# Attention values with the value block as weights: two heads' probabilities streamed, scaled by their sums before they are turned

## What is computed

```python
m = jnp.maximum(jnp.max(scores, axis=-1, keepdims=True), sink)
pexp = jnp.exp(scores - m)
probs = pexp / (jnp.sum(pexp, axis=-1, keepdims=True) + jnp.exp(sink - m))
out = jnp.einsum('bgrnqk,bnkgd->bnqgrd', probs.astype(v.dtype), vv)
```

## Time and profile before

| | us |
|---|---|
| median of three runs | 2171.71 |
| lowest, highest | 2169.91, 2173.41 |
| the profiled execution, its own time | 2171.98 |
| its span, first to last instruction | 2170.4 |

### The profile page before, as it was taken

One profiled execution on the slowest core, in us unless ns is written; L12 is line 12 of the kernel. 1 busy time (PEld: TensorE's weight loads), 2 busy tenths in 40 slices (PEclk: granted clock), 3 DMA queues, 4 the chain that ended last, 5 costly groups with the idle time before them and its releaser, 6 DMA issues. The chain is left out here.

```text
span 2170.4 us, 29183 instructions
## 1 busy us (share of the span) xinstructions
PE 2090.3 (96%) x10250; PEld 1740.3 (80%) x10250; DVE 1308.9 (60%) x1828; ACT 844.2 (39%) x1589; POOL 601.2 (28%) x604
## 2 busy tenths in 40 slices
PE   7999999979999999999979999999999999999997
PEld 6888889968878878878858888888888888878885
DVE  6854543227777767767743344558877777752523
ACT  5332221114455454454443222435444443443432
POOL 1000011135576566565610000014222222100000
PEclk9999999989999999999989999999999999999998
DMA  6223252223344343443355434322222222355343
GB/s 218 68 90 97 78 174 100 78 93 129 110 125 131 119 119 124 123 126 96 101 173 174 137 136 144 131 88 76 88 83 69 80 87 87 136 163 195 111 151 88
DMA packets 131838, 254.80 MB, mean 117 GB/s; under 512 B 25328, under 2 KB 70512, under 8 KB 131728
## 3 DMA queue, kind: packets, MB, share of 16 engines
q1 hardware_dynamic: 85584, 174.98, 25.1%
q0 software_dynamic: 15936, 57.42, 7.8%
q10 hardware_dynamic: 30208, 20.98, 3.0%
HBM read 189.63 MB, written 63.70 MB: 117 GB/s over the span
## 5 line engine op out<-in xcount | busy, mean ns | idle before, releaser
L155 PE MATMUL ps_zg<-u_hi,g_hi 128*128 128x512 f32 x448 | 185.6, 414 | 0.0
L157 PE MATMUL ps_zg<-u_hi,g_lo 128*128 128x512 f32 x448 | 176.7, 394 | 0.0
L156 PE MATMUL ps_zg<-u_lo,g_hi 128*128 128x512 f32 x448 | 175.5, 392 | 0.0
L2051 DVE TENSOR_TENSOR lt_d_lo<-lt_w_raw,lt_d_hi 128x640 fp32r<-128x640 f32 (+1 forms) x64 | 57.1, 892 | 147.4 <-ACT lt_d_hi L1776 142.3
L967 POOL TENSOR_TENSOR mx_seg<-mx_seg,mx_cbm 128x1024 f32<-128x1024 f32 x32 | 76.0, 2376 | 161.1 <-DVE mx_cbm L1124 161.1
L155 PE MATMUL lt_ps<-lt_h_hi,lt_w_hi 128*128 128x512 f32 x256 | 100.8, 394 | 15.0 <-DVE lt_h_lo L2089 13.9
L155 PE MATMUL ps_zg<-z_w,u_hi 128*128 128x512 f32 x256 | 107.7, 421 | 7.1 <-DVE mx_silu L1149 6.5
L157 PE MATMUL ps_zg<-z_w,u_lo 128*128 128x512 f32 x256 | 101.8, 398 | 0.0
L1650 POOL TENSOR_TENSOR lt_t_f<-lt_w_raw 128x512 f32<-128x512 f32 x21 | 29.1, 1385 | 261.7 <-DVE lt_t_lo L1979 260.2
L1776 ACT ACTIVATE lt_d_hi<-lt_w_raw 128x640 fp32r<-128x640 f32 (+1 forms) x64 | 50.6, 791 | 130.5 <-PE lt_ps L157 111.5
L156 PE MATMUL ps_zg<-z_w,u_hi 128*128 128x512 f32 x256 | 101.1, 395 | 0.0
(11 more groups left out here) (390 smaller groups left out, 6237.9 us busy)
## 6 DMA issues: line engine op xcount, KB each, us to landing
lt_w_raw<-in_w_up SPq DMA_DIRECT2D x44, 512.0 KB, 4.5
mx_a_row<-acs_s SPq DMA_DIRECT2D x32, 512.0 KB, 3.9
g_raw<-in_w_xbc SPq DMA_DIRECT2D x24, 512.0 KB, 3.7
tok_s<-fr_work POOLq DMA_DIRECT2D x24, 512.0 KB, 4.0
lt_sig<-gate_s SPq DMA_DIRECT2D x24, 512.0 KB, 3.6
lt_w_raw<-in_w_down SPq DMA_DIRECT2D x32, 384.0 KB, 3.2
ff_s<-lt_fo SPq DMA_DIRECT2D x21, 512.0 KB, 5.1
lt_w_raw<-in_w_down SPq DMA_DIRECT2D x32, 320.0 KB, 2.9
```

What stands on the lines that cost most here:

```text
L155: pe.matmul(dst, s_hi, m_hi, start=first, stop=False)
L156: pe.matmul(dst, s_hi, m_lo, start=False, stop=False)
L157: return pe.matmul(dst, s_lo, m_hi, start=False, stop=last)
L2051: dve.tensor_tensor(d_lo[:, m % 2, 0:n], w_raw[:, m % 2, 0:n], d_hi[:, m % 2, 0:n].bitcast(F32), ALU.subtract).then_inc(dw_lo_done, 1)
```

## The change

The value product is turned round. The value block (64 columns) becomes the weights, and the transposed probabilities of two heads (256 columns) are streamed; two such products write the partitions 0 to 63 and 64 to 127 of `ps_f`. The result has the features on the partitions, which is the form in which it is stored, so `o_tok`, its transposes (L1255) and `attention_out` go. The division by the sums can no longer come after the product as a scale per partition: it moves ahead of the transposes of the probabilities, as four `tensor_scalar` on `sc` with a pointer to each head's reciprocal sum, in `scale_probabilities`, which VectorE runs behind the state update and ahead of L1164. TensorE's wait for `exp_done` becomes one for `p_scaled`; its waits for `o_ready` go.

```diff
+            def scale_probabilities(n, keys, own):
+
+                dve.wait_ge(sink_done, n + 1)
+                own.did(dve.tensor_tensor(rden[:], sums[:], sink_e[:], ALU.add))
+                own.wait()
+                own.did(dve.reciprocal(rden[:], rden[:]))
+                own.wait()
+                for r in range(REP):
+                    ins = dve.tensor_scalar(sc[:, r, 0:keys], sc[:, r, 0:keys], rden[:, r:r + 1], None, ALU.mult)
+                ins.then_inc(p_scaled, 1)
...
-                    if not opening:
-                        attention_out(n - 1, first and c == 1)
...
                         dve.tensor_tensor(state[:], kept[:], ps_f[:], ALU.add).then_inc(state_ready, 1)
+                    scale_probabilities(n, keys, own)
                     dve.wait_ge(diag_done, n + 1)
...
-                    dve.wait_ge(sink_done, n + 1)
-                    do(dve.tensor_tensor(rden[:], sums[:], sink_e[:], ALU.add))
-                    do(dve.reciprocal(rden[:], rden[:]))
...
             def values(g, c):
 
-                pe.wait_ge(p_ready, NT * g + c + 1)
+                n = NT * g + c
+                pe.wait_ge(p_ready, n + 1)
+                if c < NT - 1:
+                    pe.wait_ge(state_ready, (NT - 1) * g + c + 1)
+                else:
+                    pe.wait_ge(o_out, n)
                 j, blocks = c % 2, 1 if c == 0 else 2
-                for r in range(REP):
-                    for b in range(blocks):
-                        block_of = c if b == j else c - 1
-                        last = pe.matmul(ps_a[:, r * HD:(r + 1) * HD], p_t[:, r, b], v_in[:, block_of % 4],
+                for b in range(blocks):
+                    block_of = c if b == j else c - 1
+                    for h in range(2):
+                        last = pe.matmul(ps_f[h * HD:(h + 1) * HD, 0:2 * P].rearrange("p (a n) -> p a n", a=2),
+                                         v_in[:, block_of % 4], p_t[:, 2 * h:2 * h + 2, b],
                                          start=(b == 0), stop=(b == blocks - 1))
                 last.then_inc(pv_done, 1)
...
-                pe.wait_ge(o_ready, n + 1)
-                if c < NT - 1:
-                    pe.wait_ge(state_ready, (NT - 1) * g + c + 1)
-                else:
-                    pe.wait_ge(o_out, n)
-                for a in range(2):
-                    last = pe.transpose(ps_f[:, a * P:(a + 1) * P], o_tok[:, a * P:(a + 1) * P], ident[:])
-                last.then_inc(o_turned, 1)
...
-                    pe.wait_ge(exp_done, n + 1)
+                    pe.wait_ge(p_scaled, n + 1)
```

More of the change, by code:

```diff
@@ L825, in mixers @@
         p_t = s.sb("p_t", [P, REP, 2, P])
-        o_tok = s.sb("o_tok", [P, REP * HD])
         o_t = s.sb("o_t", [P, 2, 2, P])
@@ L847, in mixers @@
             s.sem(n) for n in "gated sq_done v_ready r0_ready yn_ready y_turned y_out".split())
-        rotated, qk_turned, q_ready, scored, masked, max_ready, exp_done, sink_done, p_turned, p_ready, pv_done, o_ready, o_turned, o_out = (
-            s.sem(n) for n in "rotated qk_turned q_ready scored masked max_ready exp_done sink_done p_turned p_ready pv_done o_ready o_turned o_out".split())
+        rotated, qk_turned, q_ready, scored, masked, max_ready, sink_done, p_scaled, p_turned, p_ready, pv_done, o_out = (
+            s.sem(n) for n in "rotated qk_turned q_ready scored masked max_ready sink_done p_scaled p_turned p_ready pv_done o_out".split())
         dve_own, pool_own, act_own = s.sem("dve_own"), s.sem("pool_own"), s.sem("act_own")
@@ L993, in outputs @@
                 act.activation(y_t[:, j], ps_e[:].rearrange("p (a n) -> p a n", a=4), ACT.Copy).then_inc(y_out, 1)
-                act.wait_ge(o_turned, n + 1)
+                act.wait_ge(pv_done, n + 1)
                 if not opening:
@@ L1045, in group @@
                     for r in range(REP):
-                        ins = act.activation(sc[:, r, 0:keys], sc[:, r, 0:keys], ACT.Exp, bias=negm[:, r:r + 1],
-                                             accum_out=sums[:, r:r + 1])
-                    ins.then_inc(exp_done, 1)
+                        act.activation(sc[:, r, 0:keys], sc[:, r, 0:keys], ACT.Exp, bias=negm[:, r:r + 1],
+                                       accum_out=sums[:, r:r + 1])
                     act.activation(sink_e[:], mx[:, 1], ACT.Exp).then_inc(sink_done, 1)
@@ L1090, in split_gate @@
                 dve.tensor_tensor(g_lo[:, w], g_raw[:, w], g_hi[:, w].bitcast(F32), ALU.subtract).then_inc(g_lo_done, 1)
-            def attention_out(n, opening):
-                dve.wait_ge(pv_done, n + 1)
-                if not opening:
[L1096 to L1100, removed]
+            def scale_probabilities(n, keys, own):
[7 more added lines that the diff above has]
+                ins.then_inc(p_scaled, 1)
             def group(g, first, last):
@@ L1194, in _ @@
             group(NG - 1, False, True)
-            attention_out(NG * NT - 1, False)
         @block.tensor
@@ L1268, in group @@
                     pe.wait_ge(rotated, n + 1)
-                    if not opening:
-                        pe.wait_ge(o_ready, n)
                     for a in range(3):
```

## The result

| | before | after |
|---|---|---|
| median, us | 2172.29 (4 runs) | 2288.14 (4 runs) |
| lowest to highest | 2169.91 to 2173.41 | 2283.54 to 2291.47 |
| span of the profiled execution | 2170.4 | 2282.0 |

A forecast was written before the change was run, and what follows sets the result against it. TensorE, busy 602.8 of 615.0 us in the mixer stage, was taken to set the time. To 2172 us came 98 of waiting less 18 for the values (+80) and 16 for the clock: 2268 us, range 2203 to 2318.

The forecast's parts named there:

- What leaves TensorE: TensorE's queue: value product in 1.1 us instead of 1.71, 18 us gained; two transposes fewer, about 0.2 us a chunk.
- Taking turns with GpSimd: VectorE's state update and scaling: alternates with GpSimd's next-chunk work one instruction each, ending 3.5 us behind the transposes' old start.
- the sum: VectorE and GpSimd instructions laid out in turn for even and odd chunks: 3.6 us late with 0.1 us of hand-over.
- Size of the wait: TensorE ahead of the probabilities' transposes: 72 us in chunks 1 to 5, 10, 12, 4 in chunks 6, 0, 7; 98 us.
- The rival of four scalings in a row: VectorE keeps its turn at the ports through all four scalings: waits of 72 us, 2238 us in all; chance 0.20.
- The rival that they stay outside the exclusion: VectorE's scalings take 0.42 us each without excluding GpSimd: waits of 56 us, 2218 us in all; chance 0.17.
- The clock: TensorE's granted clock in the mixer stage: falls after a third of 24 long waits, 2 us each, 16 us.
- The rival that the clock falls at nearly every wait: TensorE's clock falls after 28 waits, 2 us each: 56 us instead of 16, 2308 us in all; chance 0.15.
- The step that named the queue behind `p_scaled` on TensorE: TensorE, in order: behind its wait for the scaling stand the rest of z, the values and the next chunk's gates.
- The faster rival: VectorE comes first at the ports, mean wait under 0.75 us a chunk: 2164 us; chance 0.07.

The follow-up runs named there:

- e3: The changed kernel with GpSimd's L948, L950 and L956 of the next chunk started only behind the scaling (p_scaled): 2194.38 us, ratio 1.0095.
- the turn behind five eighths: The changed kernel with TensorE transposing the probabilities behind five eighths of the next z instead of three: 2229.0 us, ratio 1.0263.

## Why the prediction was right

The forecast was 2268 us within 2203 to 2318; measured were 2288. The mechanism is the one forecast: the gain on TensorE, the wait behind turn-taking, and the clock. That the number came within 20 us is in part luck: the wait was forecast 27 us too large and the clock 26 us too small, and the two misses cancel. Point by point:

- **What leaves TensorE: right.** 18 us for the product and 6 for the transposes, if nothing waits. Both together gave 23 us. The halves of the columns overlap as those of the rows do: eight passes take 1.02 us from their start to the next matmul's. Eight passes of 128 columns over the whole array (the transposes of before, 1002.08 to 1002.88) take 0.80, so eight of 256 one after the other would take some 1.6, an estimate. The matmul ahead of the product starts 0.32 us before it, where whole-array matmuls of that size start 0.23 apart: the change of form going in costs 0.1 us at most. The Trainium skill (TensorEngine Tiling (Array Packing), Key Properties) says that a change of tiling mode drains TensorE. The trace sets no more than this 0.1 us against it.
- **Taking turns with GpSimd: right.** GpSimd's three rows stand between VectorE's instructions in the odd chunk as the sum had them, in the even one with one scaling ahead of the last in place of two, and with GpSimd held back the wait went to 22.7 us (theory 20).
- **Size of the wait: too large.** 98 us behind the old start of the turn were forecast, with the 0.2 us by which TensorE comes earlier some 104; measured 76.7. Chunks 1 to 5 waited 3.1 us each on average (3.6 + 0.2 forecast). In the odd chunk shown the four scalings took 0.94 us behind L956, not 1.2, and L948 began 2.35 us before TensorE got to the transposes, where the sum had it 1.9 before (the 2.1 of before less 0.2). Chunk 0 waited 0.7 us or less in three of four groups, 3 forecast: that term was an estimate without a row, and the poorest of all. Chunk 6 waited 2.0 (2.6 forecast).
- **The rival of four scalings in a row** falls: in ten chunks a turn was given away between them. Where three or four did run in a row, GpSimd had nothing ready, so those rows say nothing for it. Its 72 us of waiting are near the measured 76.7 by chance. The rival that they stay outside the exclusion falls too: it had them constant, and single ones took up to 1.98 us beside GpSimd, and 0.28 each out of its way.
- **The clock: right in kind, the term mis-sized.** A fall at a third of the waits, 16 us, was forecast; it came at 20 of 24, and the loss rose by 42 us, 34 of them behind these waits (1.7 us a fall, 2 forecast) and 8 more in chunk 7. The rival that the clock falls at nearly every wait had 56 us, nearer to 42 than the forecast's 16. With the measured terms the sum is: 77 for the scaling, 10 for the split z, 42 for the clock, less the 23 that the product alone gained: 106 of the 112 us between the spans. The rest, 6 us, is not assigned.
- **Missed: what stands behind the scaling in chunk 7.** The four splits of the next z (L1084) are in VectorE's queue behind it, and TensorE waited 9.9 us for them; those 8 us of the clock are lost in the same chunk. The step that named the queue behind `p_scaled` on TensorE should have done the same on VectorE.
- **The faster rival** named as its condition that VectorE come first at the ports. The experiment that forces this (e3) still waited 22.7 us, 0.7 a chunk, close to the 0.75 named, and was slower by 0.95%: the split z (11.6 us) and 4 us more of the clock, neither of which the rival had, are most of it.

## What to carry to other kernels

- Work on VectorE that is short by its rows is not short where GpSimd is at work: look at what GpSimd does at the very place, and count one of its instructions for each time that VectorE gives the turn away. A wait that holds GpSimd back behind the critical step can be worth more than the step itself (94 us here, for one line).
- Before a step is put into an engine's queue on the critical path, price the wait with the clock on top: here 1.5 times its length for waits of 3 us, and with no fall of the clock behind waits of up to 1.3. And list what stands behind the new step on its own engine in every variant of the loop, the last chunk too.
- A product turned round so that the small operand is the weights, with its outputs in two halves of the partitions in turn, was a gain of 40% of its time and of two transposes; what it needs, the scaling ahead of the product, must be paid where nothing waits for it.

## What the runs showed of the hardware

- Waits of 2 to 3.6 us between dense stretches of matmuls brought the granted clock from 2.4 to 1.2 GHz in 20 of 24 cases, for about 3 us after each. Length alone doesn't decide it: three of the four without a fall are the waits of chunk 1, 3.0 to 3.3 us long. Shorter waits did it less: of 25 of 0.5 to 2.5 us (the turn behind five eighths) 6 have a fall behind them, of 26 of up to 1.3 us (GpSimd behind the scaling) none. The kernel before alone had shown two falls in three waits of 2.1 us.
- VectorE and GpSimd take turns one instruction each, also in a row of four `tensor_scalar` with no wait between them: 4.09 us for the four in the longest case, 1.14 us with GpSimd held back.
- Float32 products with 64 columns of weights, put in turn to the lower and upper 64 partitions of `ps_f`, overlap: eight passes of 256 columns in 1.02 us, as the scores in 1.06 with halves of the rows (start to next start).
- A `tensor_scalar` with a pointer scalar on 128x256 float32 takes 0.28 us in a row of four with GpSimd held back; its mean in the changed kernel was 0.58:

```profile
L1098 DVE TENSOR_SCALAR mx_sc<-mx_sc,mx_rden 128x256 f32<-128x256 f32 x112 | 58.1, 578 | 1.0
```
